# One of four convolution column tiles on GpSimd, the other three accumulated by VectorE in a PSUM bank

## The reference

```python
def conformer_conv_group(u, dw_w, dw_b, ln_g, ln_b):
    val, gate = jnp.split(u, 2, axis=-1)
    v = val * jax.nn.sigmoid(gate)
    v = depthwise_conv(v, dw_w, dw_b, CONF_WIDTH // 2)     # 31 taps, each of 512 channels by itself
    return jax.nn.silu(layernorm(v, ln_g, ln_b))
```

## Time and profile before

| | us |
|---|---|
| median of 3 runs | 971.71 (970.23 to 973.34) |
| the profiled execution | 973.83 |
| its span, first to last instruction | 972.0 |
| TensorE busy | 893.5 (92%) |
| VectorE busy | 394.6 (41%) |
| ScalarE busy | 244.6 (25%) |
| GpSimd busy | 115.8 (12%) |

### The profile page before, as it was taken

The page is one execution under the profiler, slowest core; times in us unless marked ns, Lnnn a source line. Parts: engine busy times, 40 slices in busy tenths (PEclk is TensorE's granted clock), DMA queues, the critical chain, the costliest instruction groups (busy, mean ns, idle before and its releaser), DMA issues.

```text
span 972.0 us, 16301 instructions
## 1 busy us (share of the span) xinstructions
PE 893.5 (92%) x6198; PEld 498.3 (51%) x6199; DVE 394.6 (41%) x853; ACT 244.6 (25%) x394; POOL 115.8 (12%) x226
## 2 busy tenths in 40 slices
PE   3899999899879999999999948999987999999996
PEld 2444444445456656565656635447544544555453
DVE  2379999934652222222222234476254111111112
ACT  2312446322411111111112113046231111111112
POOL 2300000200021111111111130000002111111110
PEclk9999999999959999999999978999999999999999
DMA  9992497577589899989999984484467999999994
GB/s 350 347 380 91 165 356 259 198 278 283 193 343 392 316 425 424 416 315 417 384 429 421 394 318 173 170 310 191 173 227 276 400 425 403 425 422 428 422 428 174
DMA packets 68316, 314.46 MB, mean 324 GB/s; under 512 B 4668, under 2 KB 5088, under 8 KB 51888
## 3 DMA queue, kind: packets, MB, share of 16 engines
q1 hardware_dynamic: 54608, 275.78, 71.6%
q0 software_dynamic: 8992, 29.75, 8.4%
q10 hardware_dynamic: 4672, 8.30, 2.4%
HBM read 299.35 MB, written 14.47 MB: 323 GB/s over the span
## 4 chain that ended last, share of the span: by engine, by line
PE 50%; DMA 25%; DVE 18%; issue 3%; SPq 2%; ACT 2%; POOL 0%; DVEq 0%; ACTq 0%; POOLq 0%
PE ps L782 17%; DVE arena L1083 9%; PE ps L795 9%; PE ps L601 7%; DMA weight_ring<-in_exp_w_up 5%; DMA weight_ring<-in_exp_w_down 4%; DMA weight_ring<-in_exp_w_gate 4%; PE ps L851 3%; PE ps L889 3%; DMA hT<-in_exp_w_down 2%; DMA arena<-in_exp_w_up 2%; DMA arena<-in_exp_w_gate 2%; DMA weight_ring<-in_ev_w_in 2%; PE ps L567 2%; SPq L363 2%
## 5 line engine op out<-in xcount | busy, mean ns | idle before, releaser
L782 PE MATMUL ps<-weight_ring,arena 128*64 128x256 f32 x1792 | 201.5, 383 | 5.6 <-issue 3.3
L782 PEld LDWEIGHTS ps<-weight_ring,arena 128*64 128x64 f32 x1792 | 141.2, 138 | 73.4 <-issue 22.0
L1380 DVE TENSOR_TENSOR arena<-arena,ps 128x128 f32<-128x128 f32 x78 | 18.9, 284 | 252.0 <-PE ps L782 252.0
L567 PE MATMUL ps<-hT,weight_ring 128*128 128x512 f32 x256 | 114.8, 605 | 2.4 <-DMA weight_ring<-in_ev_w_in 2.1
L795 PE MATMUL ps<-weight_ring,arena 128*64 128x512 f32 x448 | 102.3, 597 | 2.5
L1083 DVE SCALAR_TENSOR_TENSOR arena<-arena,par 128x512 f32<-128x512 f32 x132 | 94.8, 749 | 4.0 <-DVE arena L1114 0.7
L1767 ACT ACT_TABLE_LOAD x39 | 50.0, 1283 | 131.2 <-issue 130.9
L567 PEld LDWEIGHTS ps<-hT,weight_ring 128*128 128x128 f32 x256 | 48.2, 192 | 67.1 <-issue 63.3
L782 PE MATMUL ps<-arena 128*64 128x256 f32 x704 | 78.0, 379 | 0.0
L501 PE MATMUL ps<-weight_ring,cond 128*32 128x128 f32 x1536 | 54.8, 304 | 22.0 <-DMA weight_ring<-in_ada_w 12.2
L601 PE MATMUL ps<-weight_ring,arena 128*128 128x512 f32 x160 | 70.7, 596 | 1.0 <-DVE arena L1530 0.5
(11 more groups left out here) (329 smaller groups left out, 887.4 us busy)
## 6 DMA issues: line engine op xcount, KB each, us to landing
weight_ring<-in_ada_w SPq DMA_DIRECT2D x24, 2048.0 KB, 14.8
weight_ring<-in_exp_w_gate SPq DMA_DIRECT2D x22, 2048.0 KB, 10.2
weight_ring<-in_exp_w_up SPq DMA_DIRECT2D x22, 2048.0 KB, 10.5
weight_ring<-in_exp_w_down SPq DMA_DIRECT2D x22, 2048.0 KB, 10.9
arena<-in_exp_w_gate SPq DMA_DIRECT2D x10, 2048.0 KB, 10.6
hT<-in_exp_w_down SPq DMA_DIRECT2D x10, 2048.0 KB, 10.9
arena<-in_exp_w_up SPq DMA_DIRECT2D x10, 2048.0 KB, 10.8
weight_ring<-in_ev_w_in SPq DMA_DIRECT2D x4, 2048.0 KB, 19.7
```

The lines of the kernel that those rows point to most:

```text
L567: last = mm(ps[:, m % 4, :], wide(slot)[:, k, P * j:P * j + P], hT[:, k, :], start=(k == 0), stop=(k == KD - 1))
L782: last = mm(ps[64 * fh:64 * fh + 64, bank, 0:256], xgT[:, k % 4, 64 * (k // 4):64 * (k // 4) + 64], w[:, k, 256 * fh:256 * fh + 256], star ...
```

## The change

The tap sum of column tile 1 goes to GpSimd. [...] There are 61 instructions, each waiting for the one before. The 16 first taps stand ahead of the wait for `s_in` 9 and the two transfers to `y_rows`, the other 15 behind them, and all ahead of the transfers of the modulation rows.

VectorE keeps tiles 0, 2 and 3. It takes them one after the other, and accumulates in PSUM bank 7; the last tap of a tile writes `cat`. `CONV_AT` is the same, so in a step with no tap left that may start (`STEPS.index((VAL, j)) > m`) it issues none. `s_cvd` is now raised by both engines, and TensorE and GpSimd wait for 2.

Since bank 7 is taken, the modulation chunks from the fifth to the twelfth all go to bank 6 (`ADA_BANK`).

```diff
-                bank = 6 + n % 2 if bank is None else bank
+                bank = ADA_BANK[n] if bank is None else bank
...
-            pe.wait_ge(s_cvd, 1)
+            pe.wait_ge(s_cvd, 2)
...
-            conv_done = {j: [0, 0] for j in range(JT)}
+            conv_done = [0, 0]
 
             def conv_taps(count, m):
 
+                total = ps[:, CONV_BANK, :].rearrange("p (s n) -> p s n", s=2)
                 for _ in range(count):
-                    tiles = [j for j in conv_done if STEPS.index((VAL, j)) <= m and conv_done[j][0] < TAPS_C]
-                    if not tiles:
+                    n, before = conv_done
+                    if n == len(CONV_VECTOR) * TAPS_C:
                         return
-                    j = min(tiles, key=lambda j: conv_done[j][1])
-                    w, before = conv_done[j]
-                    if w:
+                    j, w = CONV_VECTOR[n // TAPS_C], n % TAPS_C
+                    if STEPS.index((VAL, j)) > m:
+                        return
+                    if w == 0:
+                        dve.wait_ge(s_v, j + 1)
+                    if n:
                         dve.wait_ge(s_dve, before)
+                    src, wc = vpad[:, j, :, w:w + CTX], par[:, C_DWW + JT * w + j:C_DWW + JT * w + j + 1]
+                    if w == 0:
+                        tap_done = v.tensor_scalar(total, src, wc, par[:, C_DWB + j:C_DWB + j + 1], ALU.mult, ALU.add)
                     else:
-                        dve.wait_ge(s_v, j + 1)
-                    conv_done[j] = [w + 1, mark(tap(cat[:, JT + j, :], vpad, w, C_DWW, C_DWB, j))]
-
+                        dst = total if w < TAPS_C - 1 else cat[:, JT + j, :].rearrange("p (s n) -> p s n", s=2)
+                        tap_done = v.scalar_tensor_tensor(dst, src, wc, total, ALU.mult, ALU.add)
+                    conv_done[:] = [n + 1, mark(tap_done)]
...
-                    read_columns(6 + ada[0] % 2)
+                    read_columns(ADA_BANK[ada[0]])
...
+        conv_tmp = ada_part[:, 0, :]
...
+            def conv_tap(w):
+
+                total = cat[:, JT + CONV_POOL, :].rearrange("p (s n) -> p s n", s=2)
+                dst = conv_tmp.rearrange("p (s n) -> p s n", s=2) if w else total
+                col = C_DWW + JT * w + CONV_POOL
+                bias = None if w else par[:, C_DWB + CONV_POOL:C_DWB + CONV_POOL + 1]
+                ops = (ALU.mult,) if w else (ALU.mult, ALU.add)
+                link(g.tensor_scalar(dst, vpad[:, CONV_POOL, :, w:w + CTX], par[:, col:col + 1], bias, *ops))
+                if w:
+                    link(g.tensor_tensor(total, total, dst, ALU.add))
+
+            pool.wait_ge(s_v, CONV_POOL + 1)
+            for w in range(16):
+                conv_tap(w)
             pool.wait_ge(s_in, 9)
             for i in range(2):
                 g.dma_start(y_dram[E * MT + TOK * i:E * MT + TOK * i + TOK, :].rearrange("(t p) d -> p t d", p=P),
                             x[:, :, :]).then_inc(s_fill, 16)
+            for w in range(16, TAPS_C):
+                conv_tap(w)
+            pool.sem_inc(s_cvd, 1)
...
-            pool.wait_ge(s_cvd, 1)
+            pool.wait_ge(s_cvd, 2)
...
+ADA_BANK = [6, 5, 6, 7] + [6] * 8 + [7, 6, 7]
+CONV_BANK = 7
+CONV_VECTOR, CONV_POOL = (0, 2, 3), 1
```

## The result

The changed kernel takes 981.97 us (median of 4 runs, 980.54 to 984.06) against 972.08 for the kernel before (970.23 to 973.34): ratio 1.0105, 95% interval 1.0079 to 1.0131, so about 10 us slower. 981.0 was predicted. The profiled execution took 981.1 us, its span 979.3; before it was 973.83 and 972.0.

What follows compares the result with a forecast made beforehand. TensorE and VectorE were both taken as full, with only 2.3 us of TensorE holes to win. -2.3 us, +9.6 us stall and +2 us later gave +9.3 us, 981.0 against the median; range 970 to 989.

Steps and rivals of the forecast that it cites:

- The forecast case: VectorE instructions with two SBUF inputs and GpSimd's instructions wait for each other one by one: +9.3 us, 976 to 989, chance 0.43.
- The prize: After the last step, TensorE's waits of 0.99 us before the mean's product and 1.29 before L627 close: 2.3 us at most.
- The sum without exclusion: If GpSimd and VectorE do not hold each other: -2.3 us at the end, +1.2 us stall behind step 9, together -1.1.
- GpSimd's own time: Tile 1's 31 multiplications at 0.7 us and 30 additions at 1.2, with gaps 61.4 us, ending at 147.2 without contention.
- the threshold of 1.67: Time per GpSimd instruction in us below which tile 1's 61 instructions end before TensorE wants the result at 184.6 us.
- A wait of 0.7 per instruction: In steps 7 to 9, 12 VectorE instructions with two SBUF inputs each wait 0.7 us for GpSimd: 8.4 us.
- The stall of 9.6 us before the chunk of step 10: TensorE's modulation chunk waits for VectorE's read of the one shared bank: 1.2 us plus 8.4 us of VectorE delay.
- +2 us later: In steps 10 to 12, 12 more two-input VectorE instructions wait for GpSimd, mostly hidden behind TensorE's delay: 2 us added.
- The +17 us for whole waits: High end of the sum, each wait a whole GpSimd instruction and VectorE's writes to PSUM at their slowest.
- No exclusion: Rival: GpSimd and VectorE hardly hold each other in SBUF; -1.1 us, 970.6, with slow PSUM writes 972.7; chance 0.24.
- once per group: Rival: VectorE waits for GpSimd once per instruction group, four groups in steps 7 to 9; +1.3 to +4 us, chance 0.22.

## Why the prediction was right

The forecast case came: slower, by exclusion, with 981.0 predicted and 981.97 measured, inside its own range of 976 to 989. At the landmark, against before, the second chunk starts 142.13 - 133.46 = 8.7 us late (9.6 said), takes 1.3 us longer (not in the sum), and from its end to the landmark there are 61.0 us instead of 60.5, so +0.5 (-2.3 + 2 = -0.3 said). Together 10.5 where the sum had 9.3. The mechanism was right; that the time came within 1 us was in part luck, as its steps show:

- **The prize, at most 2.3 us.** Right as a bound. Of it the changed kernel has 1.4: the mean's product waits no more, and L628 waits 0.84 us for 1.29. The two kernels without contention and with a shorter convolution gain 1.0 (one tap on GpSimd) and 1.3 us (two sums) at the landmark.
- **The sum without exclusion, -1.1 us.** Right to 0.1 us at the landmark (-1.03, within the scatter of 0.3 named above), and in its stations: glu 2, glu 3, the stall. The first tap costs 0.85 instead of 0.46 as said (0.75), and PSUM nothing worth counting: 756 ns against 749, 0.2 us for 23 taps. One term was misread: the 6.68 us of the earlier trace rows do not give a distance of 0.607. VectorE's timeline before has these taps start at 110.99, 111.66 and 112.32 us, so 0.66 apart, and the eleven cost +1.3 us instead of +2.0. More taps than eleven had alternated (the earlier trace rows have 16 in 10.94 us, 0.68 apart), so the stretch from glu 2 to glu 3 still came at 29.1 us for 29.2. That is luck.
- **GpSimd's own time.** The term with the largest error. A multiplication was put at 0.7 us, nearest to the copy; it takes 1.57, between the ends 0.61 and 2.3. The addition, put at 1.2, takes 1.26. With the holds the means are 1.82 and 1.36, and the tile is done at 185.4 us, not 165. That is 61 instructions at (185.4 - 81.0 - 1.6) / 61 = 1.69 us each, just past the threshold of 1.67. It cost no wait before the mean's product, since VectorE's own last tap came later still (194.96 + 0.75). Without the holds, an estimate from 31 x 1.57 + 30 x 1.26 us and gaps of 0.09 puts its end near 175 us, still ahead of the 184.6 at which TensorE asked before. Its indirect cost is the contention in all of steps 10 to 15 instead of to 12.
- **A wait of 0.7 per instruction.** The mechanism is shown (reads hold, writes don't; taps in PSUM go free), its size was too large. In steps 7 to 9 the 12 instructions with two inputs in SBUF are 2.7 us longer than with one tap on GpSimd, the sum of the differences of their records, so 0.2 each, and not 8.4 us. Two things stood in for the rest. The small copies L1018 were not counted and lost 1.0 and 0.7 us. And the scans of step 6, held ahead of glu 2, raised the semaphore for which ScalarE waits 5.15 us, so that the coefficients of step 7 came late and L1121 started 2.7 us later. Together VectorE's read is 7.1 us late where 8.4 was said.
- **The stall of 9.6 us before the chunk of step 10.** Nearly right in the start of that chunk (142.13 us, 143.1 said), wrong in its place and its kind. Idle are 3.97 + 2.75 = 6.7 us, and more than half of it stands behind step 9, where the prediction had said that "the other chunks have a step or more between". Delay takes that slack too. The other 3.9 us are lower clock behind the stops, which the prediction did not price at all. Part of it is the same delay in another form: the 1.69 and 0.84 us lost before the second stop made that stop shorter. Only the 1.34 us behind it are on top.
- **+2 us later.** About right: from the second chunk's end to the landmark the changed kernel needs 206.43 - 145.42 = 61.0 us, the one with one tap 194.89 - 136.97 = 57.9. Of these 3.1 us, 1.59 are a wait of L619 for ScalarE and 0.84 one of L628.
- **The end of the range.** The +17 us for whole waits has no working. The terms as given, -2.3 + 1.2 + 12 + 1.5 + 2 x 1.0 / 0.7, make 15.3.

So the errors in size partly cancelled: a wait too large, against a copy, a late coefficient and a clock loss left out, and too short an end of the contention.

The Trainium skill (SBUF — State Buffer, section Who interferes with whom) is borne out for two-input VectorE instructions beside a GpSimd that reads (1224 to 1648 ns for the scan, 1224 when GpSimd only writes), and for taps with one input in SBUF (756). The same section names the case that the prediction passed over: a VectorE copy can enter a two-port mode, in which it contends with GpSimd, and the limit to a GpSimd instruction that reads SBUF is put there only on VectorE instructions with two inputs. The copies L1018 fit it, with 649 ns beside reading, 300 beside writing and 171 beside an idle GpSimd; no run here shows the mode itself. The rivals fell by the same rows. "No exclusion" is refuted by the scans; "once per group" by the group at 98.98 us of the changed kernel, in which a scan of 1224 ns took 2.17 us, the next, 665 before, 1.11, and the elementwise instruction behind them (692 before) 1.57 (VectorE's timeline):

```profile
98.98 2.17 DVE L1130 TENSOR_TENSOR_SCAN arena<-arena 128x512 f32<-128x512 f32 x1
101.08 1.11 DVE L1132 TENSOR_TENSOR_SCAN arena<-arena 128x256 f32<-128x256 f32 x1
...
103.01 1.57 DVE L1135 TENSOR_TENSOR arena<-arena 128x512 f32<-128x512 f32 x1
```

Open stays how much of the 11.5 us would be left with a GpSimd that needs 0.7 us a multiplication; no run has one.

## What to carry to other kernels

Ask first what the relieved engine is late for: here 22 of 31 taps left steps whose end TensorE sets, and the prize was 2.3 us however fast the convolution. Then price the lower clock behind a stop of TensorE next to the stop itself; here 1.3 us came on top that no term of the sum had. Before work goes to GpSimd, list every VectorE instruction of that stretch that reads two operands from SBUF, and the small copies on which another engine waits; they pay for it, inside their records, and the delay surfaces at the next buffer that is tight. Moving the tight place moved the stall and won back 4.4 of the 10.5 us; taking GpSimd's reads away won all of them.

## What the runs showed that was not expected

- A copy of 128x8 that takes 171 to 181 ns is held to up to 1.21 us beside a computing GpSimd, and up to 0.58 beside one that only writes. It is the instruction for which TensorE's chunks waited.
- GpSimd multiplies a tile of 128x512 by a column's scalar more slowly (1.57 us) than it adds two tiles (1.26), and copies one in 0.61.
- After a stop of 2.79 us TensorE's next chunk took 3.42 us instead of 1.95; with products in the stop it took 1.95. After one of 3.17 us in another kernel it took 1.96.
- Two sums in SBUF in turn bring the taps from 0.784 us apart to 0.66, which is also the distance of alternating taps in the kernel before (110.99, 111.66, 112.32 us), and not the 0.607 worked out from the earlier trace rows:

```profile
178.24 0.75 DVE L1084 SCALAR_TENSOR_TENSOR arena<-arena,par 128x512 f32<-128x512 f32 x1
178.90 0.75 DVE L1084 SCALAR_TENSOR_TENSOR ada_part<-arena,par,ada_part 128x512 f32<-128x512 f32 x1
```

These are VectorE's rows in the kernel with two sums. The 1.3 us at the landmark came with this smaller saving of 0.12 us a tap.
